# First scan chunk without a state product, an early Exp table, output low parts on VectorE, and sample states scaled as they are added

## The reference

```
a = rms_norm(h); proj = a @ w_in          # z | x,B,C | dt | u,v
SSD:  causal conv(4) on x,B,C -> SiLU -> chunked scan, 8 heads of 64, 2 groups,
      state 128, chunks of 128:  y = (C B^T * decay) (dt x)  +  exp(cum) * (C @ state)  + D*x
      state' = exp(total) * state + B^T (decay * dt x);  rms_norm(y * SiLU(z))
gMLP: u * (tril(W_s) v + b)
h += concat(ssd, gmlp) @ w_out
h += HierMoE(rms_norm(h))                 # best group of 4, best 2 of its 4 experts
h += sigmoid(rms_norm(h) @ w_pg) * rms_norm(p @ w_ple);   y = rms_norm(h)
```

## Time and profile before

| | us |
|---|---|
| median of 3 runs (lowest to highest) | 1126.4 (1124.49 to 1126.66) |
| the profiled execution | 1126.14 |
| its span, first to last instruction | 1124.2 |
| TensorE busy | 1055.3 (94%) |
| VectorE busy | 701.7 (62%) |
| ScalarE busy | 504.2 (45%) |
| Pool busy | 196.7 (17%) |
| mean granted TensorE clock | 0.968 of 2.4 GHz |

### The profile page before, as it was taken

How to read it: one execution, slowest core, us unless ns; L and a number is a source line. 1 busy time by engine, 2 the same in 40 slices (tenths; PEclk the granted TensorE clock), 3 DMA queues, 4 the chain that set the end, 5 groups by cost and what they waited for, 6 DMA issues and landing times.

```text
span 1124.2 us, 17530 instructions
## 1 busy us (share of the span) xinstructions
PE 1055.3 (94%) x6221; PEld 910.3 (81%) x6222; DVE 701.7 (62%) x1099; ACT 504.2 (45%) x872; POOL 196.7 (17%) x348
## 2 busy tenths in 40 slices
PE   7999999998999999946999999999999999999896
PEld 5777799985776788746988999898899999878685
DVE  4422575824867667256599566999946753576664
ACT  6733312033111122151588457787845652564332
POOL 3611000102233112111001000101000000065542
PEclk9999999999999999856999999999999999999998
DMA  8893400221513362157499675999966644142541
GB/s 333 269 273 73 171 1 1 76 79 56 179 61 87 109 247 85 57 179 261 140 371 372 241 278 206 384 353 384 358 237 256 239 178 168 57 168 82 166 146 56
DMA packets 71703, 209.01 MB, mean 186 GB/s; under 512 B 10863, under 2 KB 36079, under 8 KB 58730
## 3 DMA queue, kind: packets, MB, share of 16 engines
q1 hardware_dynamic: 61546, 174.02, 43.5%
q0 software_dynamic: 6512, 21.77, 5.5%
q10 hardware_dynamic: 3600, 12.62, 2.8%
HBM read 169.74 MB, written 38.65 MB: 185 GB/s over the span
## 4 chain that ended last, share of the span: by engine, by line
PE 57%; DVE 10%; issue 5%; ACT 3%; DVEq 1%; DMA 0%; POOL 0%; POOLq 0%; ACTq 0%; another core or an unknown queue 0%
PE bank L605 13%; PE bank L607 12%; PE bank L606 12%; PE bank L599 4%; DVE w_lo L1524 4%; PE bank L850 3%; PE bank L852 3%; PE bank L851 3%; PE bank L593 2%; ACT w_hi L1920 2%; PE bank L821 1%; PE bank L788 1%; DVE w_lo L1051 1%; PE bank L807 1%; PE bank L814 1%
## 5 line engine op out<-in xcount | busy, mean ns | idle before, releaser
L605 PE MATMUL bank<-w_hi,xh 128*128 128x256 f32 x768 | 220.7, 287 | 2.7 <-DVE xl L1051 2.7
L606 PE MATMUL bank<-w_lo,xh 128*128 128x256 f32 x768 | 218.4, 284 | 0.0
L607 PE MATMUL bank<-w_hi,xl 128*128 128x256 f32 x768 | 218.4, 284 | 0.0
L1524 DVE SCALAR_TENSOR_TENSOR w_lo<-raw_gu,cols,w_hi 128x512 fp32r<-128x512 f32 x264 | 178.0, 747 | 7.4 <-ACT w_hi L1920 6.3
L1920 ACT ACTIVATE w_hi<-raw_gu,cols 128x512 fp32r<-128x512 f32 x264 | 165.4, 712 | 21.1 <-PE bank L607 16.4
L605 PEld LDWEIGHTS bank<-w_hi,xh 128*128 128x128 f32 x768 | 147.9, 193 | 5.4 <-issue 3.1
L606 PEld LDWEIGHTS bank<-w_lo,xh 128*128 128x128 f32 x768 | 148.1, 193 | 0.5
L607 PEld LDWEIGHTS bank<-w_hi,xl 128*128 128x128 f32 x768 | 148.0, 193 | 0.0
L605 PE MATMUL bank<-w_hi,hid_hi 128*128 128x512 f32 x192 | 80.6, 420 | 11.6 <-DVE hid_lo L1051 11.6
L2230 POOL COPY index_u<-token_u 128x1 uint32 (+1 forms) x25 | 7.8, 311 | 428.2 <-PE bank L599 405.4
L607 PE MATMUL bank<-w_hi,hid_lo 128*128 128x512 f32 x192 | 75.3, 392 | 0.0
(11 more groups left out here) (373 smaller groups left out, 2195.6 us busy)
## 6 DMA issues: line engine op xcount, KB each, us to landing
raw_gu<-in_w_gate_up SPq DMA_DIRECT2D x64, 1024.0 KB, 4.9
raw_d<-in_w_down_rows SPq DMA_DIRECT2D x32, 1024.0 KB, 6.7
y_rows<-yb ACTq DMA_DIRECT2D x24, 512.0 KB, 6.4
raw_w<-in_w_in_blocks SPq DMA_DIRECT2D x20, 512.0 KB, 6.5
y_rows<-ones SPq DMA_DIRECT2D x16, 512.0 KB, 6.5
xr<-in_x_prompt_t SPq DMA_DIRECT2D x8, 512.0 KB, 9.2
xst<-in_x_prompt SPq DMA_DIRECT2D x8, 512.0 KB, 10.0
raw_o<-in_w_out SPq DMA_DIRECT2D x8, 512.0 KB, 3.6
```

What stands on the lines that cost most here:

```text
L605: nc.tensor.matmul(out, lh(k), rh(k), start=(k == 0), stop=False)
L606: nc.tensor.matmul(out, lh(k), rl(k), start=False, stop=False)
L607: last = nc.tensor.matmul(out, ll(k), rh(k), start=False, stop=(k == (K or len(ks)) - 1))
L1524: ins = V.scalar_tensor_tensor(out=gu_lo[:, k, :, cols_], in0=raw_gu[q // KC][:, k, :, :], scalar=gain(e, k), in1=gu_hi[:, k, :, cols_].bi ...
```

## The change

- The first tile has no product with the state: TensorE leaves out L807 for n = 0, VectorE leaves out the scaling and addition of bank 4, and `state_step(0)` copies bank 2 into the state. The memset of the state goes, and all counts of `yoff_done` and `state_ready` fall by one.
- On VectorE `front(0)` and `weights(0)` stand ahead of `dam(1)`.
- ScalarE runs a one-element Exp behind the last SiLU, ahead of `bt_evict(0)`; all four `o_high(1, j)` stand behind `decay(0)`.
- The four low parts of w_out's second half move from Pool to VectorE, between `cat_low(0)` and `state_step(1)`. The first output product waits for them one by one, where it comes to them, not for all at its start.
- `s_scale` on Pool goes; each addition of a sample state becomes four scalar_tensor_tensor of 128x128 that scale the old state by a column of `edcol` and add the product. The wait for these additions moves behind `seg`. SP loads the transposed states ahead of its wait for the low parts.
- `m_norm` on Pool multiplies by a scalar per row (tensor_scalar), not by a broadcast tensor.

```diff
@@ sp @@
+            sp.dma_start(s_tr, i["state_ssm_t"]).then_inc(s("s_tr_loaded"), 16)
             sp.wait_ge(s("o_low"), KC // 2)
...
-            sp.dma_start(s_tr, i["state_ssm_t"]).then_inc(s("s_tr_loaded"), 16)
@@ pe, inside(n) @@
-                else:
-                    pe.wait_ge(s("state_ready"), chunks_before(n) + 1)
+                elif n >= 1:
+                    pe.wait_ge(s("state_ready"), chunks_before(n))
...
-                last.then_inc(s("yoff_done"), 1)
+                if n >= 1:
+                    last.then_inc(s("yoff_done"), 1)
@@ pe, out_half(n, half) @@
-                        pe.wait_ge(s("o_low"), KC // 2)
                 for k in range(KC):
                     q, kk = k // (KC // 2), k % (KC // 2)
+                    if n == 0 and half == 0 and q == 1:
+                        pe.wait_ge(s("o_low"), kk + 1)
@@ pe, turns @@
                     state_update(updates + 3)
-                    pe.wait_ge(s("s_new"), updates + 4)
                 if n + 1 < TILES:
                     seg(n + 1)
+                if updates is not None:
+                    pe.wait_ge(s("s_new"), updates + 4)
@@ dve, y_chain(n) @@
-                dve.wait_ge(s("yoff_done"), n + 1)
...
+                if n >= 1:
+                    dve.wait_ge(s("yoff_done"), n)
...
@@ dve, state_step(n) @@
+                if n == 0:
+                    dve.wait_ge(s("cs_done"), 1)
+                    V.tensor_copy(state, bank[2][:, :]).then_inc(s("state_ready"), 1)
+                    return
@@ dve, state_add(j) @@
-                dst = s_nat[:, c, 4 * q:4 * q + 4, :]
-                dve.wait_ge(s("s_scaled"), j + 1)
+                if j == 0:
+                    dve.wait_ge(s("states_loaded"), 16 * XC)
                 dve.wait_ge(s("cs_s_done"), j + 1)
-                V.tensor_tensor(dst, bank[4 + q].rearrange("p (b n) -> p b n", b=4), dst, ALU.add).then_inc(s("s_new"), 1)
+                for b in range(4 * q, 4 * q + 4):
+                    dst = s_nat[:, c, b, :]
+                    ins = V.scalar_tensor_tensor(out=dst, in0=dst, scalar=edcol[:, c, b:b + 1], in1=bank[4 + q][:, (b - 4 * q) * N:(b - 4 * q + 1) * N],
+                                                 op0=ALU.mult, op1=ALU.add)
+                    if b == 4 * q + 3:
+                        own.wait()
+                        ins.then_inc(s("s_new"), 1)
+                    else:
+                        own.did(ins)
+            def out_low(j):
+                dve.wait_ge(s("a_high"), KC * 5 + KC // 2 + j + 1)
+                lo(wo_lo[1][:, j, :], raw_o[:, j, :], wo_hi[1][:, j, :]).then_inc(s("o_low"), 1)
@@ dve, start of the stage @@
             dam(0)
+            dve.wait_ge(s("sp_ready"), 2)
+            front(0)
+            weights(0)
             dam(1)
             own.did(V.memset(logits[:, NT, :], 0.0))
-            V.memset(state, 0.0).then_inc(s("state_ready"), 1)
...
+            dve.wait_ge(s("proj_ready"), 3 * TILES)
             for n in range(TILES + 2):
                 if 1 <= n <= TILES:
                     cat_low(n - 1)
+                if n == 1:
+                    for j in range(KC // 2):
+                        out_low(j)
@@ act @@
+            A.activation(conv_old[:, 0, 0:1], half_neg[:, 0:1], ACT.Exp).then_inc(s("exp_loaded"), 1)
             bt_evict(0)
-            o_high(1, 0)
             decay(0)
-            for j in range(1, KC // 2):
+            for j in range(KC // 2):
                 o_high(1, j)
@@ pool @@
-                G.tensor_tensor(xn[0:T, :], xt_h[n % 2][0:T, :], rh[0:T, t:t + 1].to_broadcast([T, D]), ALU.mult).then_inc(s("m_ready"), 1)
+                G.tensor_scalar(xn[0:T, :], xt_h[n % 2][0:T, :], rh[0:T, t:t + 1], None, ALU.mult).then_inc(s("m_ready"), 1)
...
```

More of the change, by code:

```diff
@@ L907, in _ @@
                     state_update(updates + 3)
-                    pe.wait_ge(s("s_new"), updates + 4)
                 if n + 1 < TILES:
                     seg(n + 1)
+                if updates is not None:
+                    pe.wait_ge(s("s_new"), updates + 4)
                 if n == TILES:
-                    pe.wait_ge(s("state_ready"), NT + 1)
+                    pe.wait_ge(s("state_ready"), NT)
                     for c in range(XC):
@@ L1290, in y_chain @@
                 T = rows(t)
-                dve.wait_ge(s("yoff_done"), n + 1)
[L1292 to L1296, removed]
+                if n >= 1:
+                    dve.wait_ge(s("yoff_done"), n)
+                    c3 = bank[4][0:T, :].rearrange("p (h q) -> p h q", h=HEADS)
+                    own.did(V.tensor_tensor(c3, c3, bc(ecum[0:T, 0, t, :], T, HEADS, HP), ALU.mult))
+                    own.wait()
+                    own.did(V.tensor_tensor(yy[0:T, :], bank[4][0:T, :], yy[0:T, :], ALU.add))
+                    own.wait()
                 dve.wait_ge(s("ydiag_done"), n + 1)
@@ L1357, in state_add @@
                 c, q = j // 2, j % 2
-                dst = s_nat[:, c, 4 * q:4 * q + 4, :]
-                dve.wait_ge(s("s_scaled"), j + 1)
+                if j == 0:
+                    dve.wait_ge(s("states_loaded"), 16 * XC)
                 dve.wait_ge(s("cs_s_done"), j + 1)
-                V.tensor_tensor(dst, bank[4 + q].rearrange("p (b n) -> p b n", b=4), dst, ALU.add).then_inc(s("s_new"), 1)
+                for b in range(4 * q, 4 * q + 4):
[3 more added lines that the diff above has]
+                    if b == 4 * q + 3:
+                        own.wait()
+                        ins.then_inc(s("s_new"), 1)
[4 more added lines that the diff above has]
+                lo(wo_lo[1][:, j, :], raw_o[:, j, :], wo_hi[1][:, j, :]).then_inc(s("o_low"), 1)
             dve.wait_ge(s("proj_done"), 3 * TILES)
             dam(0)
+            dve.wait_ge(s("sp_ready"), 2)
+            front(0)
+            weights(0)
             dam(1)
             own.did(V.memset(logits[:, NT, :], 0.0))
-            own.wait()
-            V.memset(state, 0.0).then_inc(s("state_ready"), 1)
[L1369 to L1372, removed]
+            dve.wait_ge(s("proj_ready"), 3 * TILES)
             for n in range(TILES + 2):
@@ L2198, in _ @@
                     y_rstd(n)
[L2199 to L2203, removed]
                 if n >= 1:
```

## The result

The changed kernel took 1115.72 us (median of 5 runs, 1114.26 to 1118.83) against 1126.4 us (5 runs, 1124.49 to 1129.28): a ratio of 0.9912, 95% interval 0.9886 to 0.9938. The forecast was 1118.5 us, with a range of 1114.5 to 1123.0. The profiled execution took 1114.82 us (span 1113.1, mean granted clock 0.980 instead of 0.968).

What follows compares the result with a forecast made beforehand. TensorE, busy 94% of the span, was taken as the bound, except where it waits, chiefly on VectorE at the scan stage's opening. 5.3 + 0.5 + 2.0 + 0 = 7.8 us gained gave 1118.5 us, range 1114.5 to 1123.0.

Steps and rivals of the forecast that it cites:

- the prediction's own sign: Stage from 269 us to the first expert: if not 6 to 9 us shorter, the prediction is wrong.
- three parts that it priced: Opening 5.3 us, then 0.5 and 2.0 us in the two steps after the sample; normalisation on Pool 0.
- rival 2: End of the stage: the clock fall beginning near 462 us does not recur, 3.3 us more, 1115.1 us; chance 0.11.
- Opening: Scan stage start, tile 0: diagonal addition 6.95 us earlier, but VectorE late at the second residual addition, so 5.3 us gained.
- Each sign: Opening: table load over before 271, weightings 1.3 us to 274.7, normalisation ending near 282, four 1.2 us low parts from 284.7.
- Rival 3: Low parts on VectorE cost Pool's 2.8 us each: 6.3 us of gain goes, 1124.8 us, no change; chance 0.06.
- The table load: ScalarE, opening: load hidden behind the decay products, charged 1.28 us without the skill's drain of about 1.38 us.
- Two steps after the sample: Decay products no longer wait for state additions: router 0.5 us earlier in the first step, 2.0 us in the second.
- rival 4: The 32 short state additions cost mostly fixed time: slower from 0.6 us each, 1131.5 us at 0.75 us; chance 0.05.
- Normalisation on Pool: Nine one-operand instructions at 1.9 us each, at most 17 us in a stage where Pool waits for TensorE: gain 0.
- Rival 1: Opening: clock falls in TensorE's new waits; both falls give 1123.6 us, one 1120.2 to 1121.7 us; chance 0.23.

Runs made afterwards that it cites:

- first experiment: Changed kernel with the four low parts of the output weights back on Pool: 1121.57 us, ratio to the kernel before 0.9963.
- the altered order: Changed kernel with VectorE's tile 0 normalisation ahead of tile 1's weighted inputs, third decay input behind the second residual addition: 1114.26 us, ratio to before 0.9894.

## Why the prediction was right, and where not

- *The sum.* By the prediction's own sign it failed: the stage from its first transposes to the first expert was to be 6 to 9 us shorter and is 11.37 shorter (248.90 to 237.53). The three parts that it priced, 5.3 + 0.5 + 2.0 = 7.8 us, came to 5.64 + 0.74 + 1.87 = 8.25. The other 3.1 us lie behind router 2, where it had put nothing but rival 2. The time fell inside the range because the range took that rival in.
- *Opening, 5.3 us forecast, 5.64 measured.* Each sign came, on the clock of the trace of before (0.79 less): table load over at 270.9, weightings 1.29 us ending at 274.8, normalisation ending at 282.2, four low parts in 4.61 us from 284.9. VectorE was late next, as said; TensorE waited 1.44 us instead of some 2. Rival 3 falls with the 4.61 us. Parts of it undone alone: the state product 1.75 us in tile 0's rows, the table 0.92, the low parts 7.6 with the lower clock in it. Their sum is over 5.64, with the clock in it; how they overlap is not shown.
- *The table load.* The Trainium skill ("ScalarE: Activation LUTs", What ACT_TABLE_LOAD costs) adds a drain of about 1.38 us. The one-element Exp began at 271.71, 0.02 us after the load ended at 271.69. The trace does not show the drain, and with the load back ahead of the exponentials the diagonal products came 0.92 us later, not 2.3. Leaving it out was right.
- *Two steps after the sample, 0.5 and 2.0 forecast, 0.74 and 1.87 measured.* The short additions cost the 0.27 us that I chose; rival 4 falls. The sizes are right, but I read too little from them: I priced the additions and the order as one step worth 2.5 us. With the additions and without the order the kernel is as slow as before: what the opening gained, 5.64 us at the gates, is lost again behind the waits.
- *Normalisation on Pool, 0 forecast: the step that failed.* "An operand less gives no reason for a longer one" was argued, not read; the instruction takes 2.84 to 3.49 us, the nine fill 26.6 us and not at most 17, and I had set no bound above 1.9. And I held it off the path by the tiles from 3 on, not by the last one, where Pool's queue goes on to constants that VectorE waits for. Price 1.2 us in the marks (1.07 us of it in that wait); the medians do not show it.
- *Rival 2, one fall fewer (0.11), came on top of the forecast.* The end of the stage gave 2.73 us: 3.98 from the last tile to the expert with the two-operand form (57.09 to 53.11), less 1.25 for the normalisation. Of the 3.98, about 2.8 us lie ahead of the last router, where the stretch at 193 to 200 was, and about 1.3 in that router, which ran into the stretch over the plan. This is why 1115.7 and not 1118.5. That the range held it is part luck: I put it down to another phase of the stage and had no row for it; the runs tie it to the order of the wait. A fall between 100 and 115 us stands in all four profiles with the wait ahead of `seg`, and one between 190 and 201 in three of them; of the ten with the wait behind, none has the first, and one has a short fall near 184. How a wait at 100 us makes a fall at 193 likelier is not shown, nor where the 0.39 us between router 2 and the last tile come from.
- *Rival 1, falls in the new waits (0.23).* Not in the profiles of the changed kernel. In a kernel that differs by the normalisation alone a fall over tile 0's diagonal products (6.6 to 14.1 us) came in one profile of two; with two more, at 34 and 62, it made 5 us, so the chance was not idle. The changed kernel's slower runs have a lower clock (1118.57 and 1118.83 us at 0.971 and 0.973, against 0.979 to 0.980 in the other three of that set); where in the kernel it fell is not shown.

## What to carry to other kernels

Where TensorE has work that does not need what it waits for, that work goes ahead of the wait: here one such order was worth more in clock than in waiting. An instruction's queue is followed to its end: the last turn of a loop can be on the path where all the others are hidden. Gains of 1 to 2 us are judged by marks in the trace, counted from a common start, with the clock beside them, since medians of runs hold the falls of the clock too.

## What the runs showed of the hardware that was not expected

- On Pool a 128x1024 multiplication by one value per row takes 2.85 us, by a broadcast second tensor 1.89 us: the form with an operand less is half as long again.
- Beside it VectorE's two-operand instruction is held less. In the changed kernel:

```profile
394.78 2.85 POOL L2207 TENSOR_SCALAR xn<-xt_h,rh 128x1024 f32<-128x1024 f32 x1
395.27 1.17 DVE L1330 TENSOR_TENSOR state<-state,ecum 128x512 f32<-128x512 f32 x1
```

  VectorE ends at 396.44, in the middle of Pool's instruction; in the kernel before the same state scaling took 1.89 to 2.14 us beside Pool's 1.9.
- VectorE's sums of squares go from 0.45 to 2.5 us beside Pool's two-operand instructions (first experiment).
- The clock can fall with TensorE busy in all of the four microseconds before (the altered order), and one kernel shows none or three falls from one execution to the next.
